# RWKV-7 chunk recurrence: the triangular inverse applied ahead of the recurrence, and a query output summed in PSUM

## What is computed

```
def step(state, inp):
    r_t, w_t, k_t, v_t, a_t, b_t = inp
    sa = jnp.einsum('bhvk,bhk->bhv', state, a_t)
    state = (state * w_t[:, :, None, :]
             + sa[..., None] * b_t[:, :, None, :]
             + v_t[..., None] * k_t[:, :, None, :])
    y_t = jnp.einsum('bhvk,bhk->bhv', state, r_t)
    return state, y_t
```

## Time and profile before

| what | before |
|---|---|
| runs, us | 2544.7, 2549.28, 2550.91; median 2549.28 |
| span of the profiled execution, first to last instruction | 2547.0 us |
| TensorE busy | 2224.2 us, 87% |
| VectorE, ScalarE, GpSimd busy | 1172.0, 899.3, 165.3 us |
| back of quarter 0, alone | 830.0 to 841.6 us |
| recurrence of quarters 0, 1, 2, 3, with partners | 841.6, 897.0, 951.6, 999.1 to 1056.2 us |

### The profile page before, as it was taken

The page is one execution under the profiler, slowest core; times in us unless marked ns, Lnnn a source line. Parts: engine busy times, 40 slices in busy tenths (PEclk is TensorE's granted clock), DMA queues, the critical chain, the costliest instruction groups (busy, mean ns, idle before and its releaser), DMA issues. The chain is left out here.

```text
span 2547.0 us, 32582 instructions
## 1 busy us (share of the span) xinstructions
PE 2224.2 (87%) x13786; PEld 1627.7 (64%) x13786; DVE 1172.0 (46%) x1828; ACT 899.3 (35%) x1398; POOL 165.3 (6%) x175
## 2 busy tenths in 40 slices
PE   8999999976999886799999989977897878888875
PEld 8777888855766775577888867766876333333331
DVE  4457565347465565576664341846545211111112
ACT  5344443237653222453443244644323111111111
POOL 0000000000001110000000000000420111101111
PEclk9899999988999887799999999975898899999988
DMA  5122222322210101122222323120114899999996
GB/s 204 67 78 88 85 97 90 96 87 91 83 67 13 20 15 51 58 100 83 99 88 87 107 83 124 66 67 14 30 40 188 353 419 418 409 407 401 405 411 235
DMA packets 107542, 377.27 MB, mean 148 GB/s; under 512 B 55008, under 2 KB 55792, under 8 KB 68736
## 3 DMA queue, kind: packets, MB, share of 16 engines
q1 hardware_dynamic: 85264, 294.34, 31.4%
q10 hardware_dynamic: 9744, 69.21, 6.5%
q0 software_dynamic: 12384, 11.58, 1.5%
HBM read 375.31 MB, written 27.53 MB: 158 GB/s over the span
## 5 line engine op out<-in xcount | busy, mean ns | idle before, releaser
L599 PE MATMUL ps<-xh,wh 128*128 128x512 f32 x1224 | 488.6, 399 | 61.4 <-DVE wl L563 41.5
L600 PE MATMUL ps<-xl,wh 128*128 128x512 f32 x1224 | 484.4, 396 | 0.0
L601 PE MATMUL ps<-xh,wl 128*128 128x512 f32 x1224 | 483.3, 395 | 0.0
L563 DVE TENSOR_TENSOR wl<-raw,wh 128x2048 fp32r<-128x2048 f32 (+2 forms) x123 | 255.1, 2074 | 280.3 <-ACT wh L557 280.3
L3626 PE MATMUL ps<-egu,XT 128*64 128x512 f32 x1088 | 273.8, 661 | 84.6 <-DMA egu<-e_up 79.0
L599 PEld LDWEIGHTS ps<-xh,wh 128*128 128x128 f32 x1224 | 234.6, 192 | 123.3 <-DVE wl L563 50.4
L601 PEld LDWEIGHTS ps<-xh,wl 128*128 128x128 f32 x1224 | 234.4, 191 | 50.3
L600 PEld LDWEIGHTS ps<-xl,wh 128*128 128x128 f32 x1224 | 235.1, 192 | 48.8 <-issue 0.2
L3626 PEld LDWEIGHTS ps<-egu,XT 128*64 128x64 f32 x1088 | 94.6, 151 | 240.3 <-issue 229.0
L557 ACT ACTIVATE wh<-raw 128x2048 fp32r<-128x2048 f32 (+2 forms) x123 | 212.7, 1730 | 90.4 <-PE ps L1082 69.2
L3644 DVE TENSOR_TENSOR HIDT<-ps,SIL 128x256 f32<-128x256 f32 x34 | 14.4, 425 | 351.7 <-ACT SIL L3636 351.7
(11 more groups left out here) (558 smaller groups left out, 3468.6 us busy)
## 6 DMA issues: line engine op xcount, KB each, us to landing
egu<-e_gate SPq DMA_DIRECT2D x68, 1024.0 KB, 14.1
egu<-e_up SPq DMA_DIRECT2D x68, 1024.0 KB, 24.9
ed<-e_down ACTq DMA_DIRECT2D x64, 1024.0 KB, 11.0
raw<-up SPq DMA_DIRECT2D x44, 1024.0 KB, 4.9
raw<-down SPq DMA_DIRECT2D x32, 704.0 KB, 4.1
raw<-rwkv_kr SPq DMA_DIRECT2D x8, 1024.0 KB, 4.8
raw<-in_dn SPq DMA_DIRECT2D x8, 1024.0 KB, 4.9
raw<-sgu_v SPq DMA_DIRECT2D x4, 1024.0 KB, 10.2
```

What stands on the lines that cost most here:

```text
L563: e.tensor_tensor(K.WL[s][:, 0:n], K.RAW[r][:, 0:n], K.WH[s][:, 0:n].bitcast(F32), SUB).then_inc(*K.w_low.mark(i))
L599: e.matmul(o, h[:, q, k], x_high[:, k], start=k == 0, stop=False)
L600: e.matmul(o, h[:, q, k], x_low[:, k], start=False, stop=False)
L601: last = e.matmul(o, l[:, q, k], x_high[:, k], start=False, stop=k == KT - 1)
```

## The change

At the end of each back stage the kernel now also makes `turned` (A transposed, through the identity, two groups of eight products), `w` (T times A, 32 products) and `u0` (T times X, 32 products). ScalarE copies `turned` to `TA`, which takes the place of `TN`, writes `w` over A in `AR` and `u0` over `AKV`. So U of a chunk is w·S + u0, and a chunk has two matrix steps: w·S, to which VectorE adds u0, writing straight into `VU`; and the state's new part. The query part R·S is issued behind w·S, into the PSUM bank in which the output of the chunk is then accumulated, and ScalarE copies the sum to `AR`. VectorE multiplies the old state by the decay ahead of time (`SD`), and one `scalar_tensor_tensor` per `jl` gives the new state. Chunk 0 leaves out both products with the state, which is zero, and chunk 7 the state's update. The values are copied two chunks ahead. A back stage has 14 steps instead of 12, so in quarters 0 and 1 the last two run after the recurrence's 24; in quarter 2 the empty steps are 10 instead of 12. `SOLVE_AT` has 16 places a back instead of 10. `halves(c)` returns the slices `64c:64c+64` and `64-64c:128-64c`. Waits elsewhere for the recurrence's mark "s" of chunk 7 wait for "y" instead.

The diff, cut: lines removed from the three `recur` functions are the ones printed above.

```diff
+        self.TA, _ = self.lay(cut0 + 24576, ("TA", [128, 2, 4, 128]))
...
-        self.ST, self.RH, self.VU, self.Y1, x = self.lay(
-            ring0 + 4096, ("ST", [128, 2, 64]), ("RH", [128, 2, 2, 64]), ("VU", [128, 2, 2, 2, 64]), ("Y1", [128, 2, 64]))
+        self.ST, self.SD, self.VU, x = self.lay(
+            ring0 + 4096, ("ST", [128, 2, 64]), ("SD", [128, 2, 64]), ("VU", [128, 2, 2, 2, 64]))
...
-        e.wait_ge(*K.solve_sum(q - 1, 5, 1, "TT"))
-        e.wait_ge(*K.dve_solve(q - 1, 5, 1, "TT"))
-    if q == 3:
-        e.wait_ge(*K.recur_sum(0, 7, "u"))
+        e.wait_ge(*K.solve_sum(q - 1, "u0", 1))
...
+        if l == 5:
+            for jl in range(2):
+                b = take()
+                for n in range(4):
+                    for c in range(2):
+                        last = e.matmul(K.ps[64 - 64 * c:128 - 64 * c, b, 128 * n:128 * n + 128],
+                                        K.AR[:, 0, 2 * q + jl, 128 * n + 64 * c:128 * n + 64 * c + 64], K.cst("ident", 128), start=True, stop=True)
+                last.then_inc(*K.solve_sum.mark(q, "turned", jl))
+            yield
...
-    yield from nothing(2)
+    banks = take(), take()
+    for jl in range(2):
+        e.wait_ge(*K.act_solve(q, "turned", jl))
+        e.wait_ge(*K.dve_solve(q, 5, jl, "TT"))
+        for n in range(4):
+            for c in range(2):
+                for par in range(2):
+                    p = slice(64 - 64 * c, 128 - 64 * c)
+                    at = 256 * jl + 64 * n
+                    last = e.matmul(K.ps[64 * par:64 * par + 64, banks[c], at:at + 64], K.TA[p, jl, n, 64 * par:64 * par + 64],
+                                    TT[p, 4 * (2 * jl + par) + n], start=True, stop=True)
+    last.then_inc(*K.solve_sum.mark(q, "w"))
+    yield
+    for half in range(2):
+        b = take()
+        for nl in range(2):
+            n = 2 * half + nl
+            for hl in range(4):
+                at = 128 * (hl % 2) + 64 * (hl // 2)
+                for h in (0, 64):
+                    last = e.matmul(K.ps[h:h + 64, b, 256 * nl + at:256 * nl + at + 64], TT[h:h + 64, 4 * hl + n], AKV[h:h + 64, n, at:at + 64],
+                                    start=True, stop=True)
+        last.then_inc(*K.solve_sum.mark(q, "u0", half))
+    yield
...
+    yield
+    for jl in range(2):
+        v = 8 + jl
+        e.wait_ge(*K.solve_sum(q, "turned", jl))
+        e.activation(K.TA[:, jl], bank(v).rearrange("p (n k) -> p n k", n=4), ACT.Copy).then_inc(*K.act_solve.mark(q, "turned", jl))
+        K.board.empty(("solve", SOLVE_AT[f"b{q}"] + v), K.act_solve(q, "turned", jl))
+    yield
+    yield from nothing(2)
+    e.wait_ge(*K.solve_sum(q, "w"))
+    for c in range(2):
+        v = 12 + c
+        e.activation(K.AR[:, 0, 2 * q:2 * q + 2].rearrange("p j (n c t) -> p j n c t", n=4, c=2)[:, :, :, c],
+                     bank(v).rearrange("p (j n t) -> p j n t", j=2, n=4), ACT.Copy).then_inc(*K.act_solve.mark(q, "w", c))
+        K.board.empty(("solve", SOLVE_AT[f"b{q}"] + v), K.act_solve(q, "w", c))
+    yield
+    for half in range(2):
+        v = 14 + half
+        e.wait_ge(*K.solve_sum(q, "u0", half))
+        e.activation(AKV[:, 2 * half:2 * half + 2], bank(v).rearrange("p (n k) -> p n k", n=2), ACT.Copy).then_inc(
+            *K.act_solve.mark(q, "u0", half))
+        K.board.empty(("solve", SOLVE_AT[f"b{q}"] + v), K.act_solve(q, "u0", half))
+    yield
...
 def recur_pe(K, e, q):
     z = set_of(K, q)
     K.board.point("PE", "recur", q)
     for t in K.board.all_at("recur", q):
         e.wait_ge(*t)
...
+    e.wait_ge(*K.act_solve(q, "u0", 1))
     for ch in range(8):
         n, c = ch // 2, ch % 2
...
+        _, P_ = halves(c)
         f = 64 * ch
...
+        if ch:
+            e.wait_ge(*K.dve_recur(q, "st", ch - 1))
             for jl in range(2):
...
+                for par in range(2):
+                    r = slice(64 * par, 64 * par + 64)
+                    last = e.matmul(K.ps[P_, par, 64 * jl:64 * jl + 64], K.AR[r, 0, 2 * q + jl, f:f + 64], K.ST[r, jl], start=True, stop=True)
+            last.then_inc(*K.recur_sum.mark(q, ch, "a"))
+            e.wait_ge(*K.act_recur(q, "y", ch - 1))
+            for jl in range(2):
+                for par in range(2):
+                    r = slice(64 * par, 64 * par + 64)
+                    e.matmul(K.ps[r, 2, 64 * jl:64 * jl + 64], K.ST[r, jl], K.AR[r, 1, 2 * q + jl, f:f + 64],
+                             start=jl == 0, stop=False, skip_group_check=True)
         yield
...
+        e.wait_ge(*K.dve_recur(q, "u", ch))
+        e.wait_ge(*K.act_recur(q, "v", ch))
+        if ch < 7:
             for jl in range(2):
...
+                for par in range(2):
+                    r = slice(64 * par, 64 * par + 64)
+                    at = 128 * jl + 64 * par
+                    last = e.matmul(K.ps[r, 3, 64 * jl:64 * jl + 64], turned_keys(K, q, c)[:, n, at:at + 64], K.VU[:, c, par, jl],
+                                    start=True, stop=True)
+            last.then_inc(*K.recur_sum.mark(q, ch, "s"))
+        for jl in range(2):
+            for par in range(2):
+                r = slice(64 * par, 64 * par + 64)
+                last = e.matmul(K.ps[r, 2, 64 * jl:64 * jl + 64], K.VU[:, c, par, jl], z["RKB"][:, 4 * (2 * jl + par) + n, c],
+                                start=ch == 0 and jl == 0, stop=jl == 1, skip_group_check=True)
+        last.then_inc(*K.recur_sum.mark(q, ch, "y"))
         yield
...
         yield
...
+    values(1)
     for ch in range(8):
...
         yield
...
         yield
+        e.wait_ge(*K.recur_sum(q, ch, "y"))
+        e.activation(K.AR[:, 1, 2 * q:2 * q + 2, 64 * ch:64 * ch + 64], K.ps[:, 2, 0:128].rearrange("p (j t) -> p j t", j=2),
+                     ACT.Copy).then_inc(*K.act_recur.mark(q, "y", ch))
+        if ch < 6:
+            values(ch + 2)
         yield
...
     for ch in range(8):
         n, c = ch // 2, ch % 2
...
+        _, P_ = halves(c)
+        U0 = z["AKV"][P_, n].rearrange("p (a j v) -> p a j v", a=2, j=2)
         if ch:
...
+            e.wait_ge(*K.recur_sum(q, ch, "a"))
+            e.tensor_tensor(K.VU[P_, c], K.ps[P_, 0:2, 0:128].rearrange("p a (j v) -> p a j v", j=2), U0, ADD).then_inc(
+                *K.dve_recur.mark(q, "u", ch))
+        else:
+            e.wait_ge(*K.act_solve(q, "u0", 1))
+            e.tensor_copy(K.VU[P_, c], U0).then_inc(*K.dve_recur.mark(q, "u", ch))
+        decay = K.PC[:, 2 * q:2 * q + 2, ch:ch + 1]
+        if 0 < ch < 7:
+            e.wait_ge(*K.dve_recur(q, "st", ch - 1))
+            e.tensor_tensor(K.SD[:, :, :], K.ST[:, :, :], decay.to_broadcast([128, 2, 64]), MUL).then_inc(*K.dve_recur.mark(q, "decayed", ch))
+        yield
+        if ch < 7:
+            e.wait_ge(*K.recur_sum(q, ch, "s"))
+            new = K.ps[:, 3, 0:128].rearrange("p (j v) -> p j v", j=2)
+            if ch:
+                e.wait_ge(*K.dve_recur(q, "decayed", ch))
+                for jl in range(2):
+                    last = e.scalar_tensor_tensor(K.ST[:, jl], new[:, jl], K.PC[:, 2 * q + jl, ch:ch + 1], K.SD[:, jl], MUL, ADD)
+                last.then_inc(*K.dve_recur.mark(q, "st", ch))
+            else:
+                e.tensor_tensor(K.ST[:, :, :], new, decay.to_broadcast([128, 2, 64]), MUL).then_inc(*K.dve_recur.mark(q, "st", ch))
         yield
         yield
...
-        e.wait_ge(*K.dve_recur(j // 2, "y", 7))
+        e.wait_ge(*K.act_recur(j // 2, "y", 7))
...
-        weave([recur_pe(K, e, q), chain(front_pe(K, e, q + 2) if q < 2 else nothing(12), back_pe(K, e, q + 1))], 2)
+        weave([recur_pe(K, e, q), chain(front_pe(K, e, q + 2) if q < 2 else nothing(10), back_pe(K, e, q + 1))], 2)
...
-        beside = abreast(front_dve(K, e, q + 2) if q < 2 else nothing(12), rows_dve(K, e, q + 1))
+        beside = abreast(front_dve(K, e, q + 2) if q < 2 else nothing(10), rows_dve(K, e, q + 1))
```

90 lines of the change are left out of this document (20 added, 70 removed).

## The result

The changed kernel took 2531.59 us, the median of four runs (2527.0 to 2537.12), against 2548.36 for four of the kernel before: ratio 0.9938, interval 0.992 to 0.9955. It is faster by more than the 0.3% that a measurement tells; I had forecast 2549.0 with a range from 2541. Nine further runs beside twenty of the kernel before (the first experiment) gave 2534.18 against 2545.35, ratio 0.9956, interval 0.9939 to 0.9974, so 11 us and not 17.

What follows compares the result with a forecast made beforehand. No single bound: TensorE, VectorE or the dependence chain by stage. Terms +5.6 - 0.5 - 0.5 + 6.0 - 10.8 = -0.2 us on a span of 2547.0, plus 2.3 to the median, gave 2549.0; range 2541 to 2558.

Steps and rivals of the forecast that it cites:

- Back of quarter 0, +5.6: Back stage running alone: 6.1 us of added TensorE products plus 0.7 for the last copy, less a 1.2 us gap.
- Front halves, -4.0 each: Quarters 0 and 1 beside a front: 4.0 us less over four chunks, VectorE losing 0.7 us a chunk.
- Back halves, +3.5 each: Quarters 0 and 1 beside a back: 6.1 us of products, less 1.3 for records, 0.5 gap, 0.8 waits.
- Quarter 2, +6: Quarter 2 grows by 6 us, bounds +3 and +11; its back waits for the small inverse's DMAs.
- +1.0 for rows beside GpSimd: Quarter 2's front half: one more slow VectorE row while GpSimd makes masks, delaying the small inverse's copy by 1.0 us.
- +1.5 for VectorE's late adds: Quarter 2's back half: `w` waits for VectorE's last adds, which come two steps later, 1.5 us.
- Quarter 3, -10.8: Quarter 3: 6.8 us less VectorE work and 4.0 us from T products and U copies in four chunks.
- bound of -13: Quarter 3's largest gain, 13 us, if three quarters of the T steps counted as covered show too.
- query's wait costed at nothing: Query product waits for ScalarE's output copy behind the function passes; priced at zero since VectorE is later still.
- The rest, 2.3 us to the median: Added outside the stage: 2.3 us between the profiled span of 2547.0 and the runs' median, 2549.28.
- faster rival: Whole stage: TensorE's clock and waits go the right way, -9.4 us, 2540; chance 0.18.
- slower rival: Quarter 3's back, in quarter 2: TensorE idles 9 us for DMAs, then runs at 1.2 GHz; +8.8, 2558; chance 0.23.

Runs made afterwards that it cites:

- the first experiment: The changed kernel run again with no edit, nine further runs beside twenty of the kernel before: 2534.18 us against 2545.35, ratio 0.9956.
- doubled `w`: The changed kernel with the products `w` of each back stage issued twice: 2538.76 us, ratio 0.9974.
- version without the first part: The changed kernel, but with the inverse applied in each chunk and back stages as in the kernel before: 2531.75 us, ratio 0.9944.

## Why the prediction was wrong

The reading by stage held, and so did the sign of every part. What failed is the size of the terms in the sum. It set gains and costs of some 10 us each against one another, and every term erred to the same side: quarter 2's, forecast at +6.0 and measured at +1.7, by 4.3 us; the two back halves together by 2.7; quarter 3's by 2.1; the others by 0.8 together. The stage gained 9.9 us and not 0.2. The rest of the distance from 2549.0 to 2531.59 lies outside the stage, in code that is the same in both kernels, and varies from execution to execution. Without that luck, by the nine further runs, the changed kernel takes 2534.18 us and is still below 2541.

- **Back of quarter 0, +5.6: measured +5.2.** `turned` 1.97 as taken. `w` 1.54, with a wait of 0.3 for VectorE's last add inside it, 1.20 in quarter 3's back and 1.05 for the second group of the doubled `w`, in place of 2.06: priced by a row whose products lie otherwise in the array. `u0` 2.03.
- **Front halves, -4.0 each: measured -4.1 and -4.3, for the wrong reason.** I gave 0.7 us a chunk, 2.8 of the 4, to VectorE, and the rest mostly to the T product where TensorE bounds. The version without the first part shows -0.6 and -1.4 for all of VectorE's part, and so -3.5 and -2.9 for the T product. Two errors cancelled. The earlier trace rows had TensorE at 29.4 of 36.5 us and half clock for most of it; its idle time stayed, and its busy time was the bound to price by.
- **Back halves, +3.5 each: measured +2.2 and +2.1.** Without the first part they are 1.1 shorter than before; the first part adds 3.3, against 5.3 in the lone back, since it also takes the T products out of the chunks beside the back. I had priced these at 0.032 us a record by a row of 64 that follow closely, where a group of eight spans 0.08 a record. The cheaper `w` (1.2 against 2.06) is about 0.9 of the 1.3 by which I missed. The products did not hide under waits: TensorE idles 1.3 us without them and 1.5 with them.
- **Quarter 2, +6: measured +1.7, the largest miss.** The wait is there, 7.31 us, ended by the DMA. The front half came to 25.1 and not 26.3: the copy begins 13.3 us in, 1.5 earlier than the 14.8 of before, where I had taken 0.5. My +1.0 for rows beside GpSimd did come (four of them at 0.91 to 1.00 us, where two at 1.0 and one at 0.50 stood before), so the shorter chain was worth 2.5 and not 1.5. The back half is 24.2 and not 27.9. I had put +1.5 for VectorE's late adds, and one wait of 0.98 ahead of `w` stands there; I had put +1.0 for the clock, and there was none, as the rows below show; `w` is 0.9 cheaper. By the version without the first part (25.6 and 18.7) the quarter is 3.3 us shorter by the rest of the change and 5.0 longer by the first part.
- **Quarter 3, -10.8: measured -12.9.** VectorE's busy time fell by 7.2 (38.2 to 31.1), near my 6.8, and brought 5.5. The T products and copies of U brought 7.4 and not 4.0: I counted four of eight chunks at about 1.0 us. My bound of -13 had the right case. The query's wait costed at nothing was rightly so in the one place shown above; the run that moved it does not settle it, since it brought costs of its own. The VectorE rows that go sum to 11.5 and not 11.7, which changes nothing.
- **The rest, 2.3 us to the median.** I read the profile of before as one execution and took the part ahead of the stage as fixed. It varies by 12 us between profiles of kernels that are the same there. My 0.3% bound was meant for this, but a range of 2541 to 2558 around one sum left little room for it: the stage's 9.9 alone, from 2549.28, give 2539.4.

The faster rival, with -9.4 us and 2540, is what the stage did, though by other terms (its front halves at -6 did not come). I had given it 0.18. That its sum agrees is luck in part. The slower rival's wait came without its price. The clock around it, from two windows of the changed kernel:

```profile
967.30:972.90 5.60, 5.60 (x109) 5.60 (x110) 0.72 (x2) 1.77 (x4) 0.00 (x0) 0.50 0.01 3
972.90:991.50 18.60, 16.22 (x497) 15.28 (x493) 6.68 (x18) 6.34 (x15) 0.00 (x0) 1.00 0.10 28
```

and from two of the kernel before:

```profile
978.40:983.70 5.30, 5.30 (x90) 5.18 (x88) 1.00 (x3) 1.57 (x3) 0.00 (x0) 0.50 0.01 3
983.70:998.80 15.10, 13.24 (x382) 12.49 (x379) 9.82 (x27) 3.17 (x8) 0.00 (x0) 1.00 0.01 3
```

TensorE was granted 1.2 GHz for 5.60 us behind the 7.31 us wait, and for 5.3 us behind the half-idle stretch of before. By the rule of the Trainium skill ("TensorE: Matmul & The Clock Gate", Loop structure matters more than you think) the products behind a DMA wait run cold, and they do; but they ran just as cold before, so the change paid nothing new for it. TensorE was at half clock ahead of the wait already (0.50 from 963.0 to 972.9). Where TensorE came to such a wait at full clock, the price did appear: with the return divided in every quarter the back halves of quarters 0 and 1 are 2.4 and 2.5 us longer. So the mechanism of the slower rival exists, but not in the place that it named, and not at its price.

The Trainium skill ("TensorEngine Tiling (Array Packing)", Key Properties) has a drain at each change of tiling mode, and the trace agrees that a change costs something. A narrow window at the start of `turned` in the lone back, with the last record of Z ahead of it:

```profile
827.98 0.22 PE L1813 MATMUL ps<-TN,tmp 64*64 64x64 f32 x1
828.13 0.33 PE L1821 MATMUL ps<-cst,AR 128*64 128x128 f32 x2
```

`turned` starts 0.15 us behind the last record of Z, whose 32 records start within 0.93 us (827.05 to 827.98), 0.03 apart on average. That is again about 0.1 us for the change. At two changes a back stage it is some 0.8 us for the four, an estimate from these rows; I had mentioned 2 us and counted none.

What stays open is why 64 records of `w` take 1.2 us and 64 of `u0` 2.03, and why the first part costs 5.5 us in quarter 2's back half (18.7 to 24.2) and 3.3 in the others; the 0.98 us wait ahead of `w` is one part of that.

## What to carry to other kernels

When a change trades work between stages, try each of its parts alone: here the part that gave the change its name cost 3.2 us net, won 7.4 in the one quarter with neither a front nor a back beside it, and by the stage, though not by the times, was best applied there only. Price a product by a row that lies in the array as it does, and a term by the engine that bounds its stage, not by the engine whose work it removes. When the gain is under half a per cent, measure the stage in the profile and repeat it; the part of the program that did not change can move by as much. A wait is not dear by itself: ask which clock the engine comes to it with.

## What the runs showed of the hardware

- TensorE's granted clock fell to half for stretches of 17 and 7 us between 89 and 137 us in one execution, where TensorE was busy 58.62 of 60 us, and not at all in another execution of the same code: 0.81, 0.86 and 1.00 in the three windows of 60 us above (kernel before; changed kernel again; changed kernel). The first back product came 10.3 us later in the first of them than in the last.
- Behind a wait of 5.4 us that followed a stretch at 2.4 GHz, TensorE was granted 1.2 GHz for 5.6 us of its next work (893.86 to 899.50, return divided); behind one of 7.31 us that followed a stretch at 1.2 GHz it was 5.60 us, against 5.3 us in the kernel before, which had no such wait there.
- A change between products that read 64 rows and products that read 128 moved the next start by 0.10 us at 2.4 GHz (0.38 against 0.28 us from group to group of eight records).
- 64 records of 64 by 64 products spread over both halves of rows and columns took 1.0 to 1.2 us at 2.4 GHz, where 64 that use each row half with one column half alone took 2.03 to 2.06.
- Sixteen small DMAs issued one by one on SyncE leave one every 0.5 us (957.90 to 965.46); two queues with eight each took 4.1 and 4.17 us side by side, and the product could start 2.5 us after the last issue instead of 1.3.
